# Sample keys loaded earlier and one weight subtraction moved up, in a two-layer decoder step on one core

## The reference

```python
def cross_sublayer(x, mem_k, mem_v, lp):
    hn = rms_norm(x, lp["norm_x_pre"])
    q = jnp.einsum("bsd,dhe->bshe", hn, lp["w_xq"])
    s = jnp.einsum("bshe,bmhe->bhsm", q, mem_k).astype(jnp.float32) * MEM_SCALE
    p = jax.nn.softmax(s, axis=-1).astype(mem_v.dtype)
    o = jnp.einsum("bhsm,bmhe->bshe", p, mem_v)
    y = jnp.einsum("bshe,hed->bsd", o, lp["w_xo"])
    return x + rms_norm(y, lp["norm_x_post"])
```

## Time and profile before

| | us |
|---|---|
| median of 3 runs | 1229.58 (1229.54 to 1233.3) |
| the profiled execution | 1229.58 |
| its span in the profile | 1227.9 |
| TensorE busy | 1173.3 (96%) |
| VectorE busy | 882.6 (72%) |
| ScalarE busy | 634.3 (52%) |
| POOL busy | 165.4 (13%) |

### The profile page before, as it was taken

How to read it: one execution, slowest core, us unless ns; L and a number is a source line. 1 busy time by engine, 2 the same in 40 slices (tenths; PEclk the granted TensorE clock), 3 DMA queues, 4 the chain that set the end, 5 groups by cost and what they waited for, 6 DMA issues and landing times. The chain is left out here.

```text
span 1227.9 us, 25117 instructions
## 1 busy us (share of the span) xinstructions
PE 1173.3 (96%) x9862; PEld 1076.4 (88%) x9862; DVE 882.6 (72%) x1521; ACT 634.3 (52%) x1089; POOL 165.4 (13%) x280
## 2 busy tenths in 40 slices
PE   4999999999999999999969999999999999999998
PEld 4998999999867799997959999999996779999977
DVE  5679888888867544576486998888887674448645
ACT  5574444444457544565654634444436664447454
POOL 2200101010344000023002010100013420001210
PEclk8998999999999999999989999999999999999999
DMA  8964646565657476687338657464655765667742
GB/s 214 248 185 109 184 129 180 137 181 138 184 154 222 138 203 172 189 252 280 105 86 221 191 151 217 126 182 123 186 140 155 207 197 157 187 185 227 271 156 71
DMA packets 319256, 216.08 MB, mean 176 GB/s; under 512 B 21652, under 2 KB 300544, under 8 KB 318842
## 3 DMA queue, kind: packets, MB, share of 16 engines
q1 hardware_dynamic: 302304, 166.74, 49.2%
q0 software_dynamic: 16512, 47.73, 12.3%
q10 hardware_dynamic: 330, 0.11, 0.0%
HBM read 209.31 MB, written 7.15 MB: 176 GB/s over the span
## 5 line engine op out<-in xcount | busy, mean ns | idle before, releaser
L1297 ACT ACTIVATE whi<-stage 128x2048 fp32r<-128x2048 f32 (+2 forms) x157 | 272.8, 1739 | 296.6 <-PE U L667 255.2
L1891 DVE TENSOR_TENSOR wlo<-stage,whi 128x2048 fp32r<-128x2048 f32 x138 | 315.9, 2289 | 146.5 <-ACT whi L1297 146.4
L665 PE MATMUL U<-Ahi,whi 128*128 128x264 f32 x1152 | 334.5, 290 | 7.7 <-issue 7.2
L666 PE MATMUL U<-Alo,whi 128*128 128x264 f32 x1152 | 328.8, 285 | 0.0
L667 PE MATMUL U<-Ahi,wlo 128*128 128x264 f32 x1152 | 328.1, 285 | 0.0
L665 PEld LDWEIGHTS U<-Ahi,whi 128*128 128x128 f32 x1152 | 219.5, 191 | 8.6 <-issue 7.5
L666 PEld LDWEIGHTS U<-Alo,whi 128*128 128x128 f32 x1152 | 219.6, 191 | 0.0
L667 PEld LDWEIGHTS U<-Ahi,wlo 128*128 128x128 f32 x1152 | 218.4, 190 | 0.0
L2058 DVE SCALAR_TENSOR_TENSOR acc<-uext,cwall,acc 128x256 f32<-128x256 f32 x464 | 188.6, 479 | 0.1
L665 PE MATMUL U<-Bhi,whi 128*128 128x264 f32 x384 | 108.9, 284 | 0.0
L666 PE MATMUL U<-Blo,whi 128*128 128x264 f32 x384 | 108.8, 283 | 0.0
(11 more groups left out here) (432 smaller groups left out, 2170.2 us busy)
## 6 DMA issues: line engine op xcount, KB each, us to landing
stage<-in_w_in SPq DMA_DIRECT2D x76, 1024.0 KB, 5.9
stage<-in_w_out SPq DMA_DIRECT2D x32, 1024.0 KB, 6.2
stage<-in_w_mk SPq DMA_DIRECT2D x8, 1024.0 KB, 6.0
cp<-in_cache_kv_latent POOLq DMA_DIRECT2D x64, 128.0 KB, 3.1
cp<-in_cache_kv_latent SPq DMA_DIRECT2D x64, 128.0 KB, 2.9
stage<-in_w_mv SPq DMA_DIRECT2D x8, 1024.0 KB, 5.6
Kt<-in_cache_mem_k POOLq DMA_DIRECT2D x16, 512.0 KB, 5.1
stage<-in_w_xq SPq DMA_DIRECT2D x8, 1024.0 KB, 7.0
```

Source lines behind the costliest of these rows:

```text
L665: mm(bk[:, 0:cols], whi[:, s, w], hi[:, k, :], start=(k == 0), stop=False)
L666: mm(bk[:, 0:cols], whi[:, s, w], lo[:, k, :], start=False, stop=False)
L1297: return A_(out, in_, ACT.Copy, scale=scale)
L1891: ins = V.tensor_tensor(wlo[:, s, :], stage[:, s, :], whi[:, s, :].bitcast(F32), ALU.subtract)
```

## The change

There are two edits, one in POOL's list and one in VectorE's. POOL issues the keys of batches 4 to 7 before `store_rows(7)` and waits for the end of the last memory-value unit (`unit_done.at(l, U_XQ)`, the number of units done) instead of the split of the last query unit. VectorE's subtraction for unit `U_XO + 1` moves from behind the reciprocal to between the key copies of batches 5 and 6. Nothing is added or removed.

```diff
@@ -571,10 +571,10 @@
-            store_rows(2 * MH - 1)
-            wait_apart(pool, split_hi.sem, split_hi.at(l, U_XQ + 4))
+            wait_apart(pool, unit_done.sem, unit_done.at(l, U_XQ))
             for b in range(4, NB):
                 load_keys(b)
+            store_rows(2 * MH - 1)
             load_values(6)
@@ -2473,6 +2473,8 @@
             for b in range(3, NB):
                 y_keys(b)
+                if b == 5:
+                    lo(U_XO + 1, 1)
             dve.wait_ge(ys_mm.sem, ys_mm.at(l, NB))
@@ -2485,7 +2487,6 @@
             V.reciprocal(sm[0:R, 11:12], sm[0:R, 9:10]).then_inc(yr_rdy.sem, 1)
-            lo(U_XO + 1, 1)
             dve.wait_ge(xo_hi.sem, xo_hi.at(l, MH + 1))
```

## The result

The changed kernel is slower: 1236.33 us in the median of 12 runs (1232.59 to 1240.15) against 1229.56 for the kernel before (12 runs, 1226.56 to 1233.35). The ratio is 1.0056, 95% interval 1.0043 to 1.0069, or 6.8 us. The forecast was 1232.7 us with a range from 1230.1 to 1236.2, and a chance of 0.59 for no change; the measured median lies just above the range. A second comparison on another occasion gave 1.0078 (1.0065 to 1.0090). The ratios here are estimates from all runs of both kernels, so they need not be the quotients of the medians.

A forecast was written before the change was run, and what follows sets the result against it. TensorE, with matmuls running for 96% of the span, was taken to bound the kernel. Added to 1229.58 us, 1.8 for the subtraction and 1.3 for the load's stall gave 1232.7 us, range 1230.1 to 1236.2.

The forecast's parts named there:

- The forecast's own sign for slower: SP's load of the last query unit: taking over 11.8 us makes the kernel measurably slower.
- The moved subtraction: VectorE between copies of batches 5 and 6: delays batch 6's scores 0.9 us per layer, 1.8 us in all.
- The earlier load of the last output unit: SP's load at 587.88 goes out at about 581.5, as a stage slot frees earlier: no gain, no harm.
- The keys' new place: POOL's queue: keys of batches 4 to 7 go out at 541.0 instead of 553.03, twelve us earlier.
- the threshold of 10.8: Last query unit's load: TensorE stalls only if it lands after 553.3; under 10.8 us the second term is nothing.
- The failed step: TensorE before the last query unit: load lands nearly at 554.0, stalling 0.65 us per layer, 1.3 us in all.
- the lower end, 553.1: Landing of the last query unit's load, from bytes in flight at measured rates plus fixed time: just in time, no stall.
- No term: First output unit's load, queued behind the late load on SP: costs nothing, its subtraction being wanted only at 590.
- the nearest row: SP's weight load beside four key loads and one of values, from 554.81 on: 12.3 us, implying landing at 554.8.
- second rival: TensorE before the last query unit, both layers: load queues behind the keys, 1234.4 to 1236.0 us; chance 0.25.
- The Trainium skill's fit: Transfers around the last query unit's load: 3.67 MB in by 551.5, stall nothing.
- The third rival: Less crowding at 553 to 570 and a faster TensorE clock behind the 9.4 us wait: 1229.2 us; chance 0.05.

The follow-up runs named there:

- two keys early: Kernel before with keys of batches 4 and 5 issued early, those of 6 and 7 and batch 6's values behind ScalarE's split as before: 1229.5 us, ratio 1.000.
- keys only: Kernel before with only POOL's part of the change, VectorE's subtraction where it was: 1236.9 us, ratio 1.0079; run again 1234.23 us, ratio 1.0039.
- keys behind the landing: Kernel before with keys of batches 4 to 7 waiting for the landing of the last query unit's load instead of ScalarE's split: 1229.8 us, ratio 1.0006.
- keys on SP's queue: Kernel before with keys of batches 4 to 7 issued early by SP behind the last query unit's load, batch 6's values late: 1228.94 us, ratio 1.000.

## Why the prediction was wrong

The direction in which the change pushed, both its terms and the point at which the stall begins were right; the size of one term was not, and with it the choice between no change and slower. The forecast's own sign for slower, a load of over 11.8 us, was met in layer 0.

- The moved subtraction: forecast 0.9 per layer and 1.8 in all. The profile has 0.79 at the place named, in both layers, and the run by itself 1.3 us (0.1 to 2.5). Right. What it left behind gave nothing back: VectorE's idle time before the tail grew from 2.35 to 4.54 us. Right.
- The earlier load of the last output unit (SP, 587.88 before, 584.62 after) brought no new wait. Right.
- The keys' new place (541.0 forecast, 539.97 after with a start 1.1 us shorter) and the chain from the load by way of ScalarE and VectorE to TensorE, 4.24 us long: landing near 554.9, start at 559.25. Right, and 9.4 us without a stall (two keys early) and 11.8 with one bear out the threshold of 10.8.
- **The failed step** is "I take the middle of 553.1 and 554.8, nearly 554.0: 0.65 per layer, 1.3 us". The load took 13.4 and 11.8 us, and in the other kernels with the same early keys and values 13.1 to 13.9 in layer 0 and 11.2 to 13.5 in layer 1. TensorE started the unit 2.8 us late in layer 0 and 1.1 in layer 1 of the changed kernel, 3.9 together; the two profiles of keys only lost 4.5 and 5.5 in both layers. The term is 3.9 to 5.5 instead of 1.3. With 1.6 for the subtraction that gives 5.5 to 7.1, and the ratio says 6.8 (5.3 to 8.5). The second comparison, 9.6 (8.0 to 11.1), is above that.
- Why it was too small: the lower end, 553.1, was a sum of bytes over rates, with the load's packets as the last of 3.67 MB. In the trace 4.32 MB moved from 542 until its last packet at 554.5. Queue 1 moved 1.66 MB of them, 0.6 more than the load: that is the first output unit's load, which the forecast put behind this one with "No term". By an estimate at the forecast's 393 GB/s it is 1.6 us. How the load came to be so far back is told above: nothing moved until 3.0 us after its issue, where alone it took 1.0; then, while the keys kept their queue full, it got as many packets as they, and so a seventh of their bytes (0.04 MB beside 0.29 at 548 to 549); and its last 75 packets trailed behind. The values, sent at 547.18, before the load was in, cost 1.2 us of it by the run that kept them late. Whether the size of the packets matters by itself isn't shown, since no run changed it; the output unit's load, with packets of 2 KB (0.70 MB / 341), took 12.3 us in much the same company.
- I had the nearest row, 12.3 us, and the 0.8 us that small rows add to it, 13.1 together. That end of the range was the answer in layer 0; averaging the row with a sum of rates was the error. The argument against the second rival, that the values come later here, was also wrong: they came before the load was in.
- The second rival was thus the right case, 1234.4 to 1236.0, with a chance of 0.25, though even its upper end lies 0.3 us under the measured median. Its mechanism, that the load is held up by the keys as the output weights were, was right as put.
- The Trainium skill's fit (2.0 us plus bytes over 436 GB/s, "DMA: Bandwidth & Descriptors", section "Anatomy of one DMA") is for a single transfer issued by GpSimd; the forecast used it for six in two queues and got 551.5 for the landing. The trace has 554.9. The same page's section "Queues, rings and completion order" says that an engine takes turns between queues packet by packet, and the packet counts of the two queues where both are full, 77 and 76 here and 345 and 341 in the kernel before, agree with it. The first 3.0 us, in which queue 1 moved nothing beside queue 0, don't follow from it. The rule should have had the weight that I gave to the sum of bytes.
- The third rival, by way of the clock, is excluded: a full clock between the layers gained nothing, and filling the stalls gained nothing (1.0039 with and without).
- What stays open: why the load starts 2 us later beside the keys, and why its last packets trail (with two keys early 81 packets took from 549 to 551, though POOL's queue moved only 0.06 MB then); layer 1's stall, which differs between executions (0.8 to 2.5 us as TensorE's wait), and so does the time between the cross-attentions, 527.0 to 530.2 us from the tail of the samples' output in layer 0 to the first key load in layer 1, counted in all kernels but the one with 20 added matmuls; and the two comparisons of keys only (1.0079 and 1.0039, on two chips), which differ by more than their intervals. No run here tells why. The 0.56 us gap inside layer 1's products with the values, which the profile puts down to issue, is not explained either.

No version here beats the kernel before. Three are as fast: two keys early, keys behind the landing, and keys on SP's queue.

## What to carry to other kernels

A transfer that nobody waits for is not free to start earlier: before moving it, list what is in flight in its new place and how much slack each of those has. When it goes to another queue than a load that is wanted soon, look at packets as well as bytes: here the load of small packets was held back at its start, in its middle and at its end. Count also what the delayed load will then meet, here the next unit's weights. Two key loads ahead instead of four, or all four behind the load in its own queue, cost nothing. And where a sum over rates and a measured row of nearly the same situation disagree, take the row, not the middle.

## What the runs showed of the hardware

- Two queues that were both full moved equally many packets: 77 (0.29 MB) and 76 (0.04 MB) in 1 us with packets of 3.7 and 0.5 KB, and 345 (1.28 MB) and 341 (0.70 MB) in 5 us with 3.7 and 2 KB.
- Alone, the weight load moved its first packets 1.0 us after its issue. With key loads of the other queue in flight it moved none for 2.9 to 3.1 us, in the changed kernel, with two keys early and with the values late. Its last 4% of packets then took 2.0 to 2.5 us, where alone they took under 1.
- The same load took 5.4 to 6.5 us alone, 7.9 to 9.4 with two 512 KB loads ahead, 11.9 to 12.3 with four, 13.1 to 13.9 in layer 0 and 11.2 to 13.5 in layer 1 with a fifth 7 us later, and 5.5 to 6.9 with four behind it in its own queue.
- A float32 matmul of 264 columns, written once, ran as two instructions of 0.227 us each (36 in 8.17 us); 20 of them as filler cost 9.06 us.
- Behind a wait of 9.4 us TensorE's granted clock was 0.50 at 624 to 628, and keeping it at 1.00 changed the total by nothing (1.0006, 0.9996 to 1.0016), since VectorE set the pace there. Behind stalls of 2.2 to 2.9 us in layer 0 it was 0.50 in one profile and 1.00 in three.
